# Reordering the first pooling, adaLN and first gate/up stages of a two-layer trunk on one NeuronCore

## The chip, the cores and the metric

The kernel is one program on one core of a Trainium2 chip. The metric is device time in microseconds of that core; lower is better. The time before is the median of three runs, 1387.15 us (1382.97 to 1387.4).

## The reference

The trunk has two layers over 256 tokens of width 1024. Only layer 0 up to its channel mixer matters here:

```python
mod_all = einsum('bd,lde->lbe', silu(c), w_mod) + b_mod        # 6 rows of 1024 per layer
shift1, scale1, gate1, shift2, scale2, gate2 = split(mod_all[0], 6)
h = rms_norm(x, g0) * (1 + scale1) + shift1
# pooling mixer: four groups of 256 channels, windows 2, 4, 8, 16 tokens
pooled = causal_window_mean(h, w) - h
y = (pooled @ w_grp) * pool_scale
x = x + gate1 * rms_norm(y, g1)
h = rms_norm(x, g2) * (1 + scale2) + shift2
y = swiglu(h, ffn_w_gu, ffn_w_down)                            # 1024 -> 2816 -> 1024
```

Layer 1 (differential attention, then eight experts of which two are taken) follows and is far the longer part. All values are float32. The large products are done as three passes over parts (high and low) whose sum is nearly float32.

## The kernel before, in words

Each engine runs an instruction list written out by hand, tied to the others by semaphores; there is no scheduler. Weights come through SyncE's queue (L487 to L571) in units of 128 x 2048 floats (1 MiB, two transfers of 512 KB) into a ring of six slots, `raw`; unit r may be loaded when unit r-6 has been used (`unit_done`, L451). The queue is strictly in order.

**The head.** Sixteen units (`HEAD`, L48) hold w_mod's columns for scale1 (units 0 to 3), shift1 (4 to 7), gate1 (8 to 11) and scale2 (12 to 15). VectorE multiplies each by silu(c), a value per partition, and adds it to a 128 x 1024 row sum (`head_units`, L1171: two instructions per unit). TensorE then sums over the partitions: for a column form (one value per channel on the partitions) by `column_sums` (L1683, eight products with a single moving column), for the gate's row form by two products with ones (L1764). shift2 does not pass VectorE: `shift_unit` (L1752) multiplies its four units on TensorE with silu(c) as a one-column weight, ScalarE copies the row out (L784), and eight one-column products turn it (L1785). In queue order the transfers are units 0 to 3, x (1 MiB), the pooling matrices `pool_m` (768 KB), units 4 to 7, `poolw` (1 MiB), units 8 to 11, shift2's unit 0, unit 12, shift2's units 1 to 3, units 13 to 15, then the first gate/up units 16 and 17.

**The pooling mixer.** ScalarE normalizes x (`normalize_tile`, L734). TensorE multiplies `ones` with the pooling matrices (L1712, L1713; for the shift) and the normalized x with them (L1725, L1728), eight column blocks in four banks. ScalarE scales each block out of its bank (L777), VectorE adds shift1 times the pooled ones over all 256 tokens (L1213, eight instructions of 128 x 256). GpSimd has meanwhile multiplied `poolw` by pool_scale in two instructions (L616). TensorE mixes (L1747, 32 passes), ScalarE squares, GpSimd makes the inverse roots (L606, L608), VectorE finishes the gate row (`finish_rows`, L1135) and adds to x (`residual_mixer`, L1150, L1155).

**Into the gate/up stage.** ScalarE squares and normalizes x again, TensorE turns both 128-token tiles (`turn`, L1772, eight transposes each). ScalarE modulates 512 of 2048 columns at a time (`modulate`, L790, with scale in `modc[:, 2]` and shift in `modc[:, 3]`), takes the high part (L798), and VectorE the low part (L1103). The first weight unit is split by halves between ScalarE (L788) and VectorE (L1251, L1253, L1257). `ffn_gate_up` (L1804) starts the long run of products, 96 for a step of 256 inner columns. `keep_clock` (L1678) issues products of zeros.

Of the kernel before, what the change touches and what calls it, by code (L numbers as in the profile page):

```python
# [8 lines left out]
ACT = mybir.ActivationFunctionType  # L9
AX_X = mybir.AxisListType.X  # L10
F32 = mybir.dt.float32
# [23 lines left out]
RAW = 6  # L35
SPL = 3
# [23 lines left out]
R_FFN, Q_FFN = len(HEAD), 0  # L60

# [58 lines left out]
def shape_constants():  # L120
# [31 lines left out]
def build_trunk(nc, x, c, w_mod, b_mod, norm_g, pool_w, pool_scale, w_qkv, w_o, subln_g, lambda_vecs,  # L152
# [8 lines left out]
    with ExitStack() as ctx:  # L161
# [102 lines left out]
        pool_m = scr[:, 0:4 * 384].rearrange("p (g s) -> p g s", g=4)  # L264
# [66 lines left out]
        first_lo = sem("first_lo")  # L331
        mcol_loaded = sem("mcol_loaded")
# [5 lines left out]
        m1_ps = sem("m1_ps")  # L338
# [106 lines left out]
        def _(sp):  # L445
# [47 lines left out]
            for r, (g, pair) in enumerate(HEAD):  # L493
# [83 lines left out]
        def _(pool):  # L577
# [54 lines left out]
            pool.wait_ge(col_ps, 5)  # L632
# [82 lines left out]
        def _(act):  # L715
            def high(r, q, rounds=0, qo=0):

                act.wait_ge(raw_loaded[r % RAW], 32 * (r // RAW + 1) + 32 * rounds)
# [60 lines left out]
            copy_wide(1, 6, gain[:, 1, :])  # L779
# [6 lines left out]

            act.wait_ge(raw_loaded[R_FFN % RAW], 32 * (R_FFN // RAW + 1))
            act.activation(whi[:, 0, 0:D], raw[:, R_FFN % RAW, 0:D], ACT.Copy).then_inc(hi_ready, 1)  # L788

# [68 lines left out]
            act.wait_ge(col_ready, 7)  # L858
# [31 lines left out]
            def project_high(u):  # L890
                act.wait_ge(raw_loaded[(R_WO + u) % RAW], 32 * ((R_WO + u) // RAW + 1))
# [76 lines left out]
            def expert_high(ps_no, m, e=0):  # L968

                r, q = R_MOE + ps_no * NE * EXPERT_UNITS + m, Q_MOE + ps_no * NE * EXPERT_UNITS + m  # L970
                act.wait_ge(raw_loaded[r % RAW], 32 * (r // RAW + 1) + 32 * (EXPERT_UNITS // RAW) * e)
# [115 lines left out]
        def _(dve):  # L1087
# [17 lines left out]
            def gemv_unit(r, l, g, cols, n, rounds=0, ro=0, no=0):  # L1105

                dve.wait_ge(raw_loaded[r % RAW], 32 * (r // RAW + 1) + 32 * rounds)
# [63 lines left out]
            def head_units(units):  # L1171

                for r in units:
                    g, pair = HEAD[r]
                    row = rows[:, ROW[0][g], :]
                    dve.wait_ge(raw_loaded[r % RAW], 32 * (r // RAW + 1))
# [27 lines left out]
            head_units(range(6, 8))  # L1204
# [3 lines left out]
            dve.wait_ge(m1_ps, 1)  # L1208
            for k in range(KC):
# [12 lines left out]
            dve.wait_ge(raw_loaded[last % RAW], 32 * (last // RAW + 1))  # L1222
# [11 lines left out]
            dve.wait_ge(col_ps, 3)  # L1234
            dve.tensor_tensor(modc[:, 3, :], ps[:, 0, 0:KC], cols[:, 3, :], ALU.add).then_inc(col_ready, 1)

            def scale_half(h):
# [5 lines left out]
                dve.tensor_tensor(modc[:, 2, a], modc[:, 4, a], cols[:, 7, a], ALU.mult).then_inc(col_ready, 1)  # L1243

            def low_modulated(b):
# [3 lines left out]
            scale_half(0)  # L1249
            dve.wait_ge(hi_ready, 1)  # L1250
            dve.tensor_tensor(wlo[:, 0, 0:D], raw[:, R_FFN % RAW, 0:D], whi[:, 0, 0:D].bitcast(F32), ALU.subtract).then_inc(first_lo, 1)  # L1251

            dve.tensor_copy(whi[:, 0, D:2 * D], raw[:, R_FFN % RAW, D:2 * D]).then_inc(first_hi, 1)  # L1253
            scale_half(1)
# [56 lines left out]
            dve.wait_ge(col_ps, 7)  # L1311
# [335 lines left out]
        def _(pe):  # L1647
# [592 lines left out]
```

## Time and profile before

| | us |
|---|---|
| median of three runs | 1387.15 |
| lowest, highest | 1382.97, 1387.4 |
| profiled execution, its own time | 1385.89 |
| its span in the trace | 1384.1 |
| TensorE / VectorE / ScalarE / GpSimd busy | 1350.9 / 1164.5 / 900.3 / 76.3 |
| chain that ended last | TensorE 94%, VectorE 3%, ScalarE 1%, transfers 1% |

The span is the time between first and last instruction in one profiled execution; the 1.79 us between it and the execution's own time lie around it. An engine's busy time counts its instructions only. The view of the chain follows the work back from the last instruction to what released each piece. The view of windows gives the busy time of each engine in a stretch, with the granted TensorE clock (1.00 is 2.4 GHz, 0.50 is 1.2 GHz) and what the transfers moved. A float32 product appears as two passes ("x2" for one product).

### The profile page before, as it was taken

Reading aid. Unit: us, or ns where it says so; the run is one execution under the profiler, and the core shown is the slowest. Engines: PE = TensorE matmul, PEld = TensorE weight load, DVE = VectorE, ACT = ScalarE, POOL = GpSimd, SP = SyncE. Lnnn points to the kernel's source line nnn. Section 1 sums busy time; section 2 is a strip of 40 time slices with the busy share of each in tenths; the row PEclk is TensorE's granted clock in tenths of the full one; section 3 lists DMA queues with packets and bytes.
Section 4 is the critical chain, followed back from the end, with each engine's and each line's share of the span. In section 5 each row is a group of like instructions: output and inputs, shape, how many; then the busy total and the mean of one; then the engine's idle time right before and its main releaser. Section 6 shows DMA issues by size and latency. Waiting matters only on the chain.

```text
span 1384.1 us, 19467 instructions
## 1 busy us (share of the span) xinstructions
PE 1350.9 (98%) x6873; PEld 1126.0 (81%) x6873; DVE 1164.5 (84%) x949; ACT 900.3 (65%) x748; POOL 76.3 (6%) x95
## 2 busy tenths in 40 slices
PE   6999999999899999999999999999999999999996
PEld 4499999898678888888888888888888888888885
DVE  6867778788869988888888888888888888898884
ACT  3353333556648777777777777777777777777772
POOL 3510000100210000000000000000000000000000
PEclk9899999999999999999999999999999999999998
DMA  9998889688259999999999999999999999999990
GB/s 363 407 343 284 309 310 338 241 284 324 100 181 348 411 393 359 391 379 381 363 392 393 347 400 377 378 362 390 385 347 405 381 367 379 383 387 351 412 354 33
DMA packets 210074, 475.14 MB, mean 343 GB/s; under 512 B 14976, under 2 KB 38608, under 8 KB 210016
## 3 DMA queue, kind: packets, MB, share of 16 engines
q1 hardware_dynamic: 204928, 457.76, 88.5%
q0 software_dynamic: 4944, 16.35, 3.9%
q8 instruction: 35, 0.57, 0.2%
q10 hardware_dynamic: 144, 0.26, 0.0%
q14 instruction: 23, 0.19, 0.0%
HBM read 465.39 MB, written 8.93 MB: 343 GB/s over the span
## 4 chain that ended last, share of the span: by engine, by line
PE 94%; DVE 3%; ACT 1%; DMA 1%; issue 1%; SPq 0%; DVEq 0%; POOL 0%
PE ps L1667 29%; PE ps L1669 28%; PE ps L1668 28%; PE ps L2119 2%; PE ps L1758 1%; DMA raw<-w_mod 1%; PE ps L1747 1%; PE ps L1685 1%; PE ps L1951 0%; DVE wlo L1443 0%; PE ps L2085 0%; PE ps L2076 0%; PE ps L1651 0%; DVE wlx L1443 0%; DVE hs L1392 0%
## 5 line engine op out<-in xcount | busy, mean ns | idle before, releaser
L1443 DVE TENSOR_TENSOR wlx<-raw,whx 128x2048 fp32r<-128x2048 f32 x168 | 384.8, 2292 | 97.5 <-ACT whx L980 96.7
L1443 DVE TENSOR_TENSOR wlo<-raw,whi 128x2048 fp32r<-128x2048 f32 x168 | 384.1, 2288 | 4.5 <-ACT whi L980 3.0
L980 ACT ACTIVATE whi<-raw 128x2048 fp32r<-128x2048 f32 x168 | 322.3, 1920 | 88.7 <-PE ps L1669 86.2
L980 ACT ACTIVATE whx<-raw 128x2048 fp32r<-128x2048 f32 x168 | 322.3, 1919 | 82.9 <-PE ps L1669 82.9
L1667 PE MATMUL ps<-whi,thi 128*128 128x512 f32 x516 | 207.9, 403 | 0.6 <-DVE tlo L1415 0.6
L1669 PE MATMUL ps<-whi,tlo 128*128 128x512 f32 x516 | 201.7, 391 | 0.0
L1668 PE MATMUL ps<-wlo,thi 128*128 128x512 f32 x516 | 201.3, 390 | 0.0
L1667 PE MATMUL ps<-whx,thi 128*128 128x512 f32 x460 | 179.9, 391 | 0.5 <-DVE tlo L1415 0.5
L1669 PE MATMUL ps<-whx,tlo 128*128 128x512 f32 x460 | 179.3, 390 | 0.0
L1668 PE MATMUL ps<-wlx,thi 128*128 128x512 f32 x452 | 176.0, 389 | 0.0
L1667 PE MATMUL ps<-thi,whi 128*128 128x256 f32 x480 | 136.4, 284 | 2.1 <-DVE tlo L1103 2.1
L1669 PE MATMUL ps<-thi,wlo 128*128 128x256 f32 x480 | 135.9, 283 | 0.0
L1668 PE MATMUL ps<-tlo,whi 128*128 128x256 f32 x480 | 135.9, 283 | 0.0
L1099 DVE TENSOR_TENSOR wlo<-raw,whi 128x2048 fp32r<-128x2048 f32 x44 | 99.8, 2289 | 37.5 <-ACT whi L722 37.5
L1667 PE MATMUL ps<-whi,ahi 128*128 128x512 f32 x300 | 118.1, 394 | 0.6 <-DVE alo L1103 0.6
L1669 PE MATMUL ps<-whi,alo 128*128 128x512 f32 x300 | 116.9, 390 | 0.0
L1668 PE MATMUL ps<-wlo,ahi 128*128 128x512 f32 x300 | 116.9, 390 | 0.0
L1667 PEld LDWEIGHTS ps<-whi,thi 128*128 128x128 f32 x516 | 97.0, 188 | 22.4 <-issue 2.8
L1669 PEld LDWEIGHTS ps<-whi,tlo 128*128 128x128 f32 x516 | 96.9, 188 | 21.1
L1668 PEld LDWEIGHTS ps<-wlo,thi 128*128 128x128 f32 x516 | 97.2, 188 | 18.6 <-issue 0.2
L722 ACT ACTIVATE whi<-raw 128x2048 fp32r<-128x2048 f32 x44 | 83.0, 1907 | 41.0 <-PE ps L1669 41.0
L1667 PEld LDWEIGHTS ps<-whx,thi 128*128 128x128 f32 x460 | 86.3, 188 | 20.8 <-issue 3.2
(286 smaller groups left out, 1914.2 us busy)
## 6 DMA issues: line engine op xcount, KB each, us to landing
raw<-moe_w_gu SPq DMA_DIRECT2D x448, 512.0 KB, 6.1
raw<-moe_w_down SPq DMA_DIRECT2D x224, 512.0 KB, 6.3
raw<-w_mod SPq DMA_DIRECT2D x88, 512.0 KB, 5.7
raw<-ffn_w_gu SPq DMA_DIRECT2D x44, 512.0 KB, 5.2
raw<-w_qkv SPq DMA_DIRECT2D x24, 512.0 KB, 5.4
raw<-ffn_w_down SPq DMA_DIRECT2D x22, 512.0 KB, 5.0
shift_w<-w_mod SPq DMA_DIRECT2D x8, 512.0 KB, 16.0
raw<-w_o SPq DMA_DIRECT2D x8, 512.0 KB, 5.7
```

The costliest lines, as they stand in the source:

```text
L722: act.activation(whi[:, q % SPL, :], raw[:, r % RAW, :], ACT.Copy).then_inc(hi_ready, 1)
L980: act.activation(m_hi[m % MRING], raw[:, r % RAW, :], ACT.Copy).then_inc(hi_ready, 1)
L1099: dve.tensor_tensor(wlo[:, q % SPL, :], raw[:, r % RAW, :], whi[:, q % SPL, :].bitcast(F32), ALU.subtract).then_inc(unit_done, 1)
L1443: dve.tensor_tensor(m_lo[m % MRING], raw[:, r % RAW, :], m_hi[m % MRING].bitcast(F32), ALU.subtract).then_inc(unit_done, 1)
L1667: pe.matmul(out, a_hi, b_hi, start=start, stop=False, skip_group_check=check)
L1668: pe.matmul(out, a_hi, b_lo, start=False, stop=False, skip_group_check=check)
L1669: return pe.matmul(out, a_lo, b_hi, start=False, stop=stop, skip_group_check=check)
L1685: mm = pe.matmul(out[:, k:k + 1], rows[:, ROW[l][g], k * P:k * P + P], ones[:, 0:1], start=True, stop=True)
L1747: mm = pe.matmul(ps[:, 4 + 2 * t + g // 2, (g % 2) * FC:(g % 2) * FC + FC], pooled_t[:, 2 * g + k, t * P:t * P + P], poolw[:, g, k, :], st ...
L1758: mm = pe.matmul(ps[0:1, 2 + h, :], silu_c[:, k:k + 1], shift_w[:, i, kk * D + h * 512:kk * D + h * 512 + 512], start=(k == 0), stop=(k == ...
L2119: mm = pe.transpose(ps[:, 6, jj * P:jj * P + P], actf[:, jj * P:jj * P + P], ident)
```

## The change

- The pooling matrices keep only what is needed: per window 160 columns (144 for the first tile's tokens and the 16 after it, 16 for the edge), 320 KB instead of 768 KB. A column block's pooling takes three products (144, 16 and 112 columns) instead of two (256 and 128). It no longer waits for the finished scale columns, only its last bank does, and the products of ones are moved behind it and cover 16 tokens per group.
- The pooled shift is added for the first 16 tokens only, since behind them a window's mean of a constant less the constant is zero.
- VectorE's small work for lambda and ScalarE's Exp move ahead; shift1's units follow in another order around the scale columns. Head unit 12 moves behind the residual.
- The spread of the first gain goes to banks 2 and 3 and ahead of the shift's sums. pool_scale is folded in eight instructions, by group.
- The gate's sum goes ahead of all four shift units. Both turns follow the shift; shift2's columns are made with scale2's, by halves.
- Unit 16 comes in four transfers of 256 KB by halves, ScalarE takes the high part of units 16 and 17 by halves, VectorE the low part by halves; VectorE's cast is gone. shift2's unit 3 is loaded behind head unit 13.

```diff
+REACH = 16
...
-    pool = np.zeros((P, len(WINDOWS), S + P), np.float32)
+    pool = np.zeros((P, len(WINDOWS), P + 2 * REACH), np.float32)
-        pool[:, g, 0:S] = full[0:P]
-        pool[:, g, S:] = full[P:, P:]
+        pool[:, g, 0:P + REACH] = full[0:P, 0:P + REACH]
+        pool[:, g, P + REACH:] = full[P:, P:P + REACH]
...
-                    for i in range(1, 4):
+                    for i in range(1, 3):
                         load_shift(i)
+                if r == 13:
+                    load_shift(3)
...
-            load(R_FFN, 0, gu_unit(w_gu, FF, 0, 0))
+            sp.wait_ge(unit_done, R_FFN - RAW + 1)
+            first_dst = raw[:, R_FFN % RAW, :].rearrange("p (k g j) -> p k g j", k=4, g=2)
+            first_src = w_gu.rearrange("(k p) (g f) -> p k g f", p=P, g=2)
+            for i in range(2):
+                for g in range(2):
+                    sp.dma_start(first_dst[:, 2 * i:2 * i + 2, g, :], first_src[:, 2 * i:2 * i + 2, g, 0:FC]).then_inc(first_loaded[i], 16)
             load(R_FFN + 1, 0, gu_unit(w_gu, FF, 0, 1))
...
-            for ch in range(2):
-                pool.tensor_tensor(poolw[:, :, ch, :], poolw[:, :, ch, :], rows[:, 6, :].rearrange("p (g e) -> p g e", g=4),
-                                   ALU.mult).then_inc(scale_folded, 1)
+            for g in range(4):
+                for ch in range(2):
+                    pool.tensor_tensor(poolw[:, g, ch, :], poolw[:, g, ch, :], rows[:, 6, g * FC:g * FC + FC],
+                                       ALU.mult).then_inc(scale_folded, 1)
...
             copy_wide(0, 2, rows[:, 6, :])
+            act.wait_ge(lam_prod, 2)
+            act.activation(lam[:, 2:4], lam[:, 0:2], ACT.Exp).then_inc(lam_exp, 1)
+            act.preload_act_table(ACT.Silu)
             square_x(0)
             for t in range(T):
                 normalize_tile(0, t)
-            act.wait_ge(lam_prod, 2)
-            act.activation(lam[:, 2:4], lam[:, 0:2], ACT.Exp).then_inc(lam_exp, 1)
-            act.preload_act_table(ACT.Silu)
...
-            copy_wide(1, 6, gain[:, 1, :])
+            copy_wide(1, 2, gain[:, 1, :])
...
-                act.wait_ge(col_ready, 4 + b // 2)
+                a = slice(b % 2 * D, b % 2 * D + D)
+                r = R_FFN + b // 2
+                if b < 2:
+                    act.wait_ge(first_loaded[b], 32)
+                else:
+                    act.wait_ge(raw_loaded[r % RAW], landed(r))
+                half = act.activation(whi[:, b // 2, a], raw[:, r % RAW, a], ACT.Copy)
+                if b % 2:
+                    half.then_inc(hi_ready, 1)
+                else:
+                    half.then_inc(first_hi, 1)
+                act.wait_ge(col_ready, 4 + 2 * (b // 2))
                 modulate(b)
                 high_modulated(b)
-                if b == 1:
-                    high(R_FFN + 1, 1)
...
-            head_units(range(0, 6))
-            dve.wait_ge(cols_ready, 1)
-            scale_columns(0, 1, ps[:, 7, 0:KC]).then_inc(col_ready, 1)
+            head_units(range(0, 3))
...
-            head_units(range(6, 8))
+            head_units(range(3, 5))
+            dve.wait_ge(cols_ready, 1)
+            scale_columns(0, 1, ps[:, 7, 0:KC]).then_inc(col_ready, 1)
+            head_units(range(5, 8))
...
-                dve.scalar_tensor_tensor(pooled_t[:, k, :], ps[:, 2 + g // 2, (g % 2) * S:(g % 2) * S + S], modc[:, 1, k:k + 1],
-                                         pooled_t[:, k, :], ALU.mult, ALU.add).then_inc(pooled_done, 1)
-            head_units(range(8, 13))
+                dve.scalar_tensor_tensor(pooled_t[:, k, 0:REACH], ps[:, 4, KC + g * REACH:KC + g * REACH + REACH], modc[:, 1, k:k + 1],
+                                         pooled_t[:, k, 0:REACH], ALU.mult, ALU.add).then_inc(pooled_done, 1)
+            head_units(range(8, 12))
             finish_rows(0, (2,))
             residual_mixer()
-            head_units(range(13, 15))
+            head_units(range(12, 15))
...
+            def half_columns(h):
                 a = slice(4 * h, 4 * h + 4)
-                dve.wait_ge(col_ps, 4 + h)
-                dve.scalar_tensor_tensor(modc[:, 4, a], ps[:, 1 + 2 * h, 0:4], 1.0, cols[:, 4, a], ALU.add, ALU.add).then_inc(col_step, 1)
+                dve.wait_ge(col_ps, 3 + h)
+                dve.scalar_tensor_tensor(modc[:, 4, a], ps[:, 1 + 2 * h, 4:8], 1.0, cols[:, 4, a], ALU.add, ALU.add).then_inc(col_step, 1)
+                dve.tensor_tensor(modc[:, 3, a], ps[:, 1 + 2 * h, 0:4], cols[:, 3, a], ALU.add).then_inc(col_ready, 1)
                 dve.wait_ge(col_step, 2 + h)
...
+            half_columns(0)
+            low_half(0, first_lo)
             low_modulated(0)
-            dve.wait_ge(first_hi, 1)
-            dve.tensor_tensor(wlo[:, 0, D:2 * D], raw[:, R_FFN % RAW, D:2 * D], whi[:, 0, D:2 * D].bitcast(F32),
-                              ALU.subtract).then_inc(unit_done, 1)
+            half_columns(1)
+            low_half(1, unit_done)
             low_modulated(1)
-            low(R_FFN + 1, 1)
+            low_half(2, first_lo)
             low_modulated(2)
+            low_half(3, unit_done)
             low_modulated(3)
...
-            pe.wait_ge(wide_ready, 1)
             pe.wait_ge(pool_loaded[0], 16)
-            for g in range(4):
-                b, c0 = 2 + g // 2, (g % 2) * S
-                pe.matmul(ps[:, b, c0:c0 + S], ones, pool_m[:, g, 0:S], start=(g % 2 == 0), stop=False, skip_group_check=True)
-                mm = pe.matmul(ps[:, b, c0 + P:c0 + S], ones, pool_m[:, g, S:S + P], start=False, stop=True, skip_group_check=True)
-            mm.then_inc(m1_ps, 1)
-            pe.wait_ge(dist_ready, 2)
-            pe.wait_ge(col_ready, 1)
             pe.wait_ge(h_ready, T)
             for b in range(4):
-                for t in range(T):
-                    for k in (2 * b, 2 * b + 1):
-                        c0 = (k % 2) * S
-                        g = k // 2
-                        if t == 0:
-                            mm = pe.matmul(ps[:, 4 + b, c0:c0 + S], hs[:, 0, k * P:k * P + P], pool_m[:, g, 0:S],
-                                           start=(k % 2 == 0), stop=False, skip_group_check=True)
-                        else:
-                            mm = pe.matmul(ps[:, 4 + b, c0 + P:c0 + S], hs[:, 1, k * P:k * P + P], pool_m[:, g, S:S + P],
-                                           start=False, stop=True, skip_group_check=True)
+                if b == 1:
+                    pe.wait_ge(dist_ready, 2)
+                elif b == 2:
+                    pe.wait_ge(cols_ready, 1)
+                elif b == 3:
+                    pe.wait_ge(col_ready, 1)
+                for k in (2 * b, 2 * b + 1):
+                    c0 = (k % 2) * S
+                    g = k // 2
+                    pe.matmul(ps[:, 4 + b, c0:c0 + P + REACH], hs[:, 0, k * P:k * P + P], pool_m[:, g, 0:P + REACH],
+                              start=(k % 2 == 0), stop=False, skip_group_check=True)
+                    pe.matmul(ps[:, 4 + b, c0 + P:c0 + P + REACH], hs[:, 1, k * P:k * P + P], pool_m[:, g, P + REACH:P + 2 * REACH],
+                              start=False, stop=False, skip_group_check=True)
+                    mm = pe.matmul(ps[:, 4 + b, c0 + P + REACH:c0 + S], hs[:, 1, k * P:k * P + P], pool_m[:, g, REACH:P],
+                                   start=False, stop=True, skip_group_check=True)
                 mm.then_inc(pooled_ps, 1)
...
+            pe.wait_ge(wide_ready, 1)
+            pe.wait_ge(first_gain_loaded, 16)
+            spread(1, 2)
+            pe.wait_ge(pooled_ready, KC)
+            for g in range(4):
+                pe.matmul(ps[:, 4, KC + g * REACH:KC + g * REACH + REACH], ones, pool_m[:, g, 0:REACH], start=True, stop=True)
             pe.wait_ge(unit_done, 8)
-            pe.wait_ge(pooled_ready, KC)
             column_sums(0, 0, ps[:, 4, 0:KC])
-            pe.wait_ge(first_gain_loaded, 16)
-            spread(1, 6)
-            pe.wait_ge(scale_folded, 2)
             for t in range(T):
                 if t == 0:
                     pe.wait_ge(col_ready, 2)
-                else:
-                    pe.wait_ge(wide_ready, 2)
                 for g in range(4):
-                    pe.wait_ge(pooled_done, 2 * g + 2)
...
-            shift_unit(0)
             pe.wait_ge(unit_done, 12)
             for h in range(2):
                 mm = pe.matmul(bank(ROW_BANK[0][2] + h), ones, rows[:, 2, h * 512:h * 512 + 512], start=False, stop=True)
             mm.then_inc(row_ps, 1)
-            for i in range(1, 4):
+            pe.wait_ge(wide_ready, 2)
+            for i in range(4):
                 mm = shift_unit(i)
             mm.then_inc(shift_ps, 1)
...
-            turn(0)
+            for t in range(T):
+                turn(t)
             pe.wait_ge(shift_copied, 1)
-            pe.wait_ge(row_done, done_rank(0, 2))
-            for k in range(KC):
-                mm = pe.matmul(ps[:, 0, k:k + 1], rows[0:1, 3, k * P:k * P + P], ones[0:1, 0:1], start=True, stop=True)
-            mm.then_inc(col_ps, 1)
             pe.wait_ge(zeros_ready, 1)
             keep_clock(2, 8)
-            turn(1)
-            keep_clock(2, 8)
+            pe.wait_ge(row_done, done_rank(0, 2))
             for h in range(2):
+                for k in range(4):
+                    pe.matmul(ps[:, 1 + 2 * h, k:k + 1], rows[0:1, 3, (4 * h + k) * P:(4 * h + k) * P + P], ones[0:1, 0:1],
+                              start=True, stop=True)
                 if h == 0:
                     pe.wait_ge(half_sum, 1)
                 else:
                     pe.wait_ge(unit_done, len(HEAD))
                 for k in range(4):
-                    mm = pe.matmul(ps[:, 1 + 2 * h, k:k + 1], rows[:, 4, (4 * h + k) * P:(4 * h + k) * P + P], ones[:, 0:1],
+                    mm = pe.matmul(ps[:, 1 + 2 * h, 4 + k:5 + k], rows[:, 4, (4 * h + k) * P:(4 * h + k) * P + P], ones[:, 0:1],
                                    start=True, stop=True)
                 mm.then_inc(col_ps, 1)
-            keep_clock(2, 24)
+            keep_clock(2, 16)
...
-                    if first and kh == 0:
-                        pe.wait_ge(first_lo, 1)
+                    if first:
+                        pe.wait_ge(first_lo, kh + 1)
```

In `ffn_gate_up` of the first step the waits go by halves of both units instead of by halves of the first.

## Rows read from the trace of the kernel before

**Rows 1.** Windows from 77 us: busy us (count) per engine, clock, DMA share, GB/s

```profile
77.00:1381.00 1304.00, 1288.42 (x6622) 1087.74 (x6622) 1110.04 (x887) 873.22 (x707) 41.45 (x51) 0.99 0.92 341
```

**Rows 2.** Windows inside the head, the same columns

```profile
34.40:38.40 4.00, 3.06 (x19) 2.59 (x20) 1.07 (x4) 0.79 (x2) 4.00 (x2) 0.97 1.03 420
...
38.40:45.00 6.60, 6.60 (x14) 4.11 (x14) 6.42 (x10) 1.01 (x1) 3.63 (x5) 0.50 1.04 396
...
68.80:72.20 3.40, 3.40 (x24) 3.34 (x22) 0.84 (x3) 0.26 (x1) 2.76 (x4) 0.51 1.09 385
```

**Rows 3.** Chain that ended last, by time, to 38 us: start, us, what

```profile
25.77 0.85 PE ps L1712 x2
...
28.84 1.10 PE ps L1725 x4
...
30.39 0.87 PE ps L1725 x4
...
34.35 0.85 ACT ysb L777 x2
...
35.34 1.92 PE ps L1685 x16
...
37.26 2.80 PE ps L1696 x4
```

**Rows 4.** Timeline to 41 us: start, us, engine, line, operation [idle before it]

```profile
19.43 3.57 PE L1685 MATMUL ps<-consts,rows 128*128 128x1 f32 x16 [0.82 <-DVE rows L1184]
...
21.27 2.19 ACT L737 ACTIVATE hs<-xs,rstd 128x1024 f32<-128x1024 f32 x2
...
33.10 1.28 DVE L1184 SCALAR_TENSOR_TENSOR rows<-raw,silu_c,rows 128x1024 f32<-128x1024 f32 x1
...
33.64 5.25 POOL L616 TENSOR_TENSOR scr<-scr,rows 128x1024 f32<-128x1024 f32 x2 [11.44 <-DMA scr<-pool_w]
...
37.49 3.23 DVE L1213 SCALAR_TENSOR_TENSOR ysb<-ps,modc,ysb 128x256 f32<-128x256 f32 x8
...
40.64 0.74 DVE L1182 TENSOR_SCALAR rows<-raw,silu_c 128x1024 f32<-128x1024 f32 x1
```

**Rows 5.** Chain, 40 to 66 us

```profile
40.06 9.54 PE ps L1747 x32
...
49.60 3.52 PE ps L1758 x8
...
53.12 1.91 PE ps L1766 x4
...
55.04 10.39 PE ps L1758 x24
```

**Rows 6.** Timeline of VectorE, 49 to 70 us

```profile
49.55 1.28 DVE L1184 SCALAR_TENSOR_TENSOR rows<-raw,silu_c,rows 128x1024 f32<-128x1024 f32 x1
...
55.08 1.23 DVE L1135 TENSOR_TENSOR rows<-ps,gain 128x1024 f32<-128x1024 f32 x1 [2.26 <-PE ps L1766]
...
68.85 0.75 DVE L1232 SCALAR_TENSOR_TENSOR rows<-raw,silu_c,rows 128x512 f32<-128x512 f32 x1
```

**Rows 7.** Chain, 65 to 78 us

```profile
65.46 1.10 PE ps L1777 x8
...
66.55 1.91 PE ps L1786 x16
...
70.76 0.85 PE ps L1681 x8
...
72.86 0.17 DVE modc L1241
...
76.39 0.61 DVE tlo L1103
...
77.14 0.36 PE ps L1667
```

**Rows 8.** Timeline of ScalarE at the first modulation

```profile
73.26 1.02 ACT L793 ACTIVATE tmp<-ps,modc 128x256 f32<-128x256 f32 x2 [4.20 <-DVE modc L1243]
```

More of the change, by code:

```diff
@@ L60, with landed @@
 R_FFN, Q_FFN = len(HEAD), 0
+def landed(r):
+    return 32 * (r // RAW + 1) - (32 if r % RAW == R_FFN % RAW and r >= R_FFN else 0)
 def ffn_steps():
@@ L331, in build_trunk @@
         first_lo = sem("first_lo")
+        first_loaded = [sem(f"first_loaded{i}") for i in range(2)]
         mcol_loaded = sem("mcol_loaded")
@@ L716, in high @@
             def high(r, q, rounds=0, qo=0):
-                act.wait_ge(raw_loaded[r % RAW], 32 * (r // RAW + 1) + 32 * rounds)
+                act.wait_ge(raw_loaded[r % RAW], landed(r) + 32 * rounds)
                 if q >= SPL - 1:
@@ L857, in _ @@
             square_residual(1)
-            act.wait_ge(col_ready, 7)
+            act.wait_ge(col_ready, 8)
             for t in range(T):
@@ L890, in project_high @@
             def project_high(u):
-                act.wait_ge(raw_loaded[(R_WO + u) % RAW], 32 * ((R_WO + u) // RAW + 1))
+                act.wait_ge(raw_loaded[(R_WO + u) % RAW], landed(R_WO + u))
                 if u:
@@ L970, in expert_high @@
                 r, q = R_MOE + ps_no * NE * EXPERT_UNITS + m, Q_MOE + ps_no * NE * EXPERT_UNITS + m
-                act.wait_ge(raw_loaded[r % RAW], 32 * (r // RAW + 1) + 32 * (EXPERT_UNITS // RAW) * e)
+                act.wait_ge(raw_loaded[r % RAW], landed(r) + 32 * (EXPERT_UNITS // RAW) * e)
                 if ps_no == 0 and m < SPL:
@@ L1105, in gemv_unit @@
             def gemv_unit(r, l, g, cols, n, rounds=0, ro=0, no=0):
-                dve.wait_ge(raw_loaded[r % RAW], 32 * (r // RAW + 1) + 32 * rounds)
+                dve.wait_ge(raw_loaded[r % RAW], landed(r) + 32 * rounds)
                 row = rows[:, ROW[l][g], :]
@@ L1175, in head_units @@
                     row = rows[:, ROW[0][g], :]
-                    dve.wait_ge(raw_loaded[r % RAW], 32 * (r // RAW + 1))
+                    dve.wait_ge(raw_loaded[r % RAW], landed(r))
                     if pair:
@@ L1207, in _ @@
             dve.wait_ge(col_ready, 2)
-            dve.wait_ge(m1_ps, 1)
             for k in range(KC):
@@ L1212, in _ @@
                 g = k // 2
-                dve.scalar_tensor_tensor(pooled_t[:, k, :], ps[:, 2 + g // 2, (g % 2) * S:(g % 2) * S + S], modc[:, 1, k:k + 1],
-                                         pooled_t[:, k, :], ALU.mult, ALU.add).then_inc(pooled_done, 1)
-            head_units(range(8, 13))
+                dve.scalar_tensor_tensor(pooled_t[:, k, 0:REACH], ps[:, 4, KC + g * REACH:KC + g * REACH + REACH], modc[:, 1, k:k + 1],
+                                         pooled_t[:, k, 0:REACH], ALU.mult, ALU.add).then_inc(pooled_done, 1)
+            head_units(range(8, 12))
             finish_rows(0, (2,))
             residual_mixer()
-            head_units(range(13, 15))
+            head_units(range(12, 15))
             last = len(HEAD) - 1
             row, unit = rows[:, 4, :], raw[:, last % RAW, :]
-            dve.wait_ge(raw_loaded[last % RAW], 32 * (last // RAW + 1))
+            dve.wait_ge(raw_loaded[last % RAW], landed(last))
             dve.wait_ge(unit_done, last)
@@ L1233, in _, with low_half @@
                                      ALU.mult, ALU.add).then_inc(unit_done, 1)
-            dve.wait_ge(col_ps, 3)
-            dve.tensor_tensor(modc[:, 3, :], ps[:, 0, 0:KC], cols[:, 3, :], ALU.add).then_inc(col_ready, 1)
-            def scale_half(h):
+            def half_columns(h):
                 a = slice(4 * h, 4 * h + 4)
-                dve.wait_ge(col_ps, 4 + h)
-                dve.scalar_tensor_tensor(modc[:, 4, a], ps[:, 1 + 2 * h, 0:4], 1.0, cols[:, 4, a], ALU.add, ALU.add).then_inc(col_step, 1)
+                dve.wait_ge(col_ps, 3 + h)
+                dve.scalar_tensor_tensor(modc[:, 4, a], ps[:, 1 + 2 * h, 4:8], 1.0, cols[:, 4, a], ALU.add, ALU.add).then_inc(col_step, 1)
+                dve.tensor_tensor(modc[:, 3, a], ps[:, 1 + 2 * h, 0:4], cols[:, 3, a], ALU.add).then_inc(col_ready, 1)
                 dve.wait_ge(col_step, 2 + h)
                 dve.tensor_tensor(modc[:, 2, a], modc[:, 4, a], cols[:, 7, a], ALU.mult).then_inc(col_ready, 1)
+            def low_half(b, done):
+                a = slice(b % 2 * D, b % 2 * D + D)
+                if b % 2:
+                    dve.wait_ge(hi_ready, b // 2 + 1)
+                else:
+                    dve.wait_ge(first_hi, b // 2 + 1)
+                dve.tensor_tensor(wlo[:, b // 2, a], raw[:, (R_FFN + b // 2) % RAW, a], whi[:, b // 2, a].bitcast(F32),
+                                  ALU.subtract).then_inc(done, 1)
             def low_modulated(b):
@@ L1741, in _ @@
                     pe.wait_ge(col_ready, 2)
-                else:
-                    pe.wait_ge(wide_ready, 2)
                 for g in range(4):
-                    pe.wait_ge(pooled_done, 2 * g + 2)
+                    pe.wait_ge(scale_folded, 2 * g + 2)
+                    pe.wait_ge(pooled_done, KC if t == 0 and g == 0 else 2 * g + 2)
                     for k in range(2):
@@ L1813, in ffn_gate_up @@
                         k = 4 * kh + kk
-                        if first and k == 2:
-                            pe.wait_ge(unit_done, r + 1)
+                        if first and kk == 2:
+                            pe.wait_ge(unit_done, r + kh + 1)
                         if first and k % 2 == 0:
```

16 lines of the change are left out of this document (4 added, 12 removed).

## The prediction, made before the changed kernel was run

> **What bounds the kernel now.** I read the windows first. From 77 us to the end TensorE is busy for 1288 of 1304 us at a granted clock of 0.99, with the transfers at 92% [rows 1]. No line after 77 us is edited except three semaphore numbers, so the change can only move the moment at which the first gate/up product starts, 77.14 us [rows 7], and how smoothly the first 96 products follow. The transfers have slack there (341 GB/s against the 420 they reach in the head [rows 1, 2]), and an earlier start should be kept to the end.
>
> The chain of waits is read next, since the head has no single owner. Up to 26 us the transfers and the sums paced by them lead; then pooling, column sums, the gain's spread and mixing on TensorE [rows 3, 5]; shift2's 32 passes with the gate's sum between them [rows 5]; turns and column products [rows 7]; and last VectorE, which splits a weight half and casts another before it may do tlo, and TensorE waits for that until 77.14 [rows 7]. The windows show what else is at work: TensorE's clock stands at 0.50 (1.2 GHz) from about 38.1 to 45.0 and again over 68.8 to 72.2 [rows 2]. Before the first fall TensorE had idled a little over a microsecond and then done 16 one-column passes and passes with a one-partition weight [rows 3]; before the second, eight transposes and 16 one-column passes [rows 7]. One more slow stretch is visible in durations only: at 25.77 two passes of 256 columns take 0.85 us, while from 28.84 four take 0.87 to 1.10 [rows 3]. So the first pooling products ran at 1.2 GHz and the later ones at 2.4.
>
> **The change part by part.** Times are those of the profiled execution, whose own time is 1385.89 us (span 1384.1), 1.26 below the median shown.
>
> *Pooling starts earlier.* Ones times the pooling matrices stood ahead of it on TensorE [rows 3]. Now it may start when ScalarE has normalized both tiles, 23.46 [rows 4], and the scale's column sums end: 19.43 + 3.57 = 23.0 [rows 4], plus about 0.4 for lambda's products, which now go ahead of unit 3. ScalarE's Exp and its two table loads move into its idle time before x lands and cost nothing; without that cover they would cost some 3 us. Start: 23.6 instead of 28.84.
>
> *Pooling gets longer.* No row shows a product of 16 columns. One-column passes cost 3.57/16 = 0.22 us slow and 1.92/16 = 0.12 fast [rows 3, 4], which is the weight load, and a 256-column pass 0.43 or 0.22. I take 0.12 for passes of 16 and 112 columns and 144 columns likewise; slow 0.22 to 0.24. 48 passes: 5.8 us fast, 11 slow (before: 5.5). With the clock rising at about 28, as it did, 4.3 us are slow and the rest fast: the end is at 31.4 instead of 34.3. Bounds: 29.4 and 34.6.
>
> *Spread, edge products, sums.* The spread (2.80, partly slow [rows 3]) is 1.7 fast and 3.4 slow; the new edge products are 8 passes, 1.0 or 1.8. Both stand ahead of shift1's column sums now. Unit 7, whose last sum ended at 34.38 [rows 4], comes about 1.1 us earlier with the smaller transfer, some 33.0, so it does not hold them. 31.4 + 1.7 + 1.0 = 34.1; sums 1.9 to 3.6: end 36.0 to 37.7 against 37.26. This is where most of the 5.2 us go: the queue of TensorE got longer ahead of VectorE's wait.
>
> *Shift on 16 tokens.* 3.23 us [rows 4] become eight instructions at the 0.17 us of a column instruction [rows 7], 1.4 us. No row has 16 columns from PSUM at this line: bounds 1.2 and 3.2. VectorE starts unit 8 at 39.1 instead of 40.64 [rows 4]: 1.5 us earlier.
>
> *Fold by group.* 5.25 us [rows 4] in eight parts; with a fixed price between 0 and 0.6 each it ends at 38 to 42. Mixing, 9.54 us before [rows 5], starts at 39.1 and ends at 47 to 49, ahead of unit 11 (49.3): hidden.
>
> *Gate's sum ahead.* Unit 12 leaves and shift_unit(0) no longer stands before the sum. Units 8 to 11 took 10.2 us, from 40.64 to the end of L1184 at 50.83 [rows 4, 6], and now end at 49.3. The sum runs at 49.3 to 51.3, so the gate row is made at 51.4 instead of 55.08 [rows 6], 3.7 us earlier; unit 12's 2.1 us are paid behind the residual. Units 13 to 15 so end 1.6 us earlier: 68.0 instead of 69.6 [rows 6]. The transfers allow it: pool_w landed at 33.64 [rows 4], now about 1.1 earlier (448 KB less at 410 GB/s); 12 units of 1.05 MB are loaded after it up to unit 15 in either kernel, 30.7 us, so unit 15 lands near 63.2 and is wanted at 65.0.
>
> *shift2.* TensorE does the same 36 passes as before, 3.52 + 1.91 + 10.39 = 15.8 us [rows 5], from 49.3 instead of 49.60: ready at 65.1 instead of 65.43. Only 0.3 us are won on the step that all the rest queues behind.
>
> *Behind it.* Row copied at 66.1; second tile normalized at 67.3 (it stands behind that copy on ScalarE), turned by 68.4; zeros 0.5; 16 one-column passes 1.9: 70.8 against 72.86 [rows 7]. Column arithmetic 0.5, modulation and high part 1.02 + 0.63 [rows 8], tlo 0.61 [rows 7], waits between them 0.3: first product at 73.9. The wlo half and the halves after it lie beside ScalarE's work, each half (1.04 and 1.22 us) shorter than the 2.9 us of 24 products. Against 77.14 this is 3.2 us.
>
> *TensorE's own queue.* Before that product it must still do the second half's 16 passes (1.9) and 16 products of zeros (1.0; [rows 7] show 0.85 for eight, slow): 70.8 + 2.9 = 73.7, just in time. But 32 one-column passes now stand in one block, where before 8 us held turns and zeros between two blocks of 16. Both falls shown came behind such passes. If the clock falls half-way, the rest costs 0.22 a pass and the zeros double: 1 to 1.5 us. I take 1.1.
>
> The sum: -3.2 + 1.1 = -2.1 us. Own time 1383.8; against the median 1385.0.
>
> A rule speaks against the new order. The Trainium skill (TensorE: Matmul & The Clock Gate, Part 4) says transposes do not count as work for the clock. The row at hand is mixed: over 68.8 to 72.2 TensorE did eight transposes and eight products of zeros, and the clock was back at 72.2. By that rule the two turns would not hold the clock and it would fall ahead of all 32 column passes; that is the second rival.
>
> **The rivals.** *The clock holds* and is up early in pooling: the 1.1 us are not paid, and up to 2 us more come from pooling, limited by unit 15's landing. -3.2 to -5.2: 1382.5. For it: one kernel's runs of 1383 and 1387 us leave room for a clock that falls at different places from run to run. *The clock falls before the column block:* 32 passes at 0.22 are 7.1 us from 68.9, zeros 2.0: 78.0, later than 77.14, and some slow products: 1388.5. For it: the fall at 68.8 with just such work; against: the second turn now comes right before. *The transfers hold:* units 14 and 15 come late because unit 16 asks four issues and unit 13 waits less; VectorE's end stays at 69.6: no gain, 1387. Against: 1.8 us of slack by the rate above. *Slower:* pooling's passes, a third of them 16 columns wide, do not raise the clock from 1.2 GHz. They stream for only about two thirds of the time, where the 256-column passes that stood there streamed all of it. Then pooling ends at 34.6, spread and edge 5.2 later, sums at 43.4; VectorE is 4.4 us later than before at unit 8 instead of 1.5 earlier, shift2 ends near 71, and the products start 5 us late: 1392. It decides when the clock is still low after 31 us.
>
> **How the numbers follow.** Forecast 0.35, clock holds 0.27, falls before the block 0.14, transfers 0.09, slower 0.15. A measurement can tell about 0.3%, 4.2 us. Below 1383.0 lie most of "holds" and a tail of the forecast: 0.30. Above 1391.3 lies "slower" with 0.14. Within: 0.56. The range leaves out that last case and reaches to 1380.8 (holds, with its best bound and a microsecond of scatter) and up to 1389.5.
>
> **What would show it.** Right: pooling from 23.6 with 0.12 us passes after a rise near 28 (a rise after 31 is the slower rival); VectorE's eight shift instructions under 1.5 us; L1135's successor near 51.4; shift2's last pass near 65; first gate/up product at 73.5 to 76. A window at 0.50 between 68 and 76 decides between forecast and rivals; a wait of VectorE for w_mod at units 14 or 15 speaks for the transfers. Wrong: gate/up products with gaps of over 0.5 us after the first, or a difference that arises after 90 us.

## The result, and the profile of the changed kernel

The changed kernel takes 1390.62 us (median of eight runs, 1389.5 to 1393.03), the kernel before in the same comparison 1385.66 us (median of eight, 1382.55 to 1387.4). The ratio is 1.0041, 95% interval 1.003 to 1.0052: slower by 0.4%, about 5 us. The forecast was 1385.0, 2.1 below the median of three that it started from; the range ended at 1389.5. So 2.1 us less were forecast, and 5 us more were measured.

The chain that ended last, in order of time: start, us, what. Pooling's first and last product, then what stands behind it.

```profile
23.61 0.82 PE ps L1748 x2
24.43 0.24 PE ps L1750 x2
24.66 0.59 PE ps L1752 x2
...
33.25 0.51 PE ps L1748 x2
...
34.59 3.71 PE ps L1723 x4
38.29 1.82 PE ps L1762 x8
40.11 3.41 PE ps L1712 x16
...
55.12 1.98 PE ps L1791 x4
57.11 13.84 PE ps L1784 x32
70.97 1.00 ACT rows L801
...
78.54 0.92 PE ps L1708 x16
79.56 0.36 PE ps L1694
...
81.07 0.21 PE ps L1695
...
92.79 0.91 PE ps L1701 x16
```

A column block costs 0.51 + 0.24 + 0.59 = 1.34 us once under way, the last (from 33.25 to 34.59) as well: the clock never leaves 1.2 GHz in pooling. That is read from durations: the column of the granted clock shows 1.00 here, as the last section says. The durations fit the level of 0.50: the column sums' one-column passes take 0.21 us each, and e4 shows 0.22 for such a pass in a window that does read 0.50. Pooling lasts from 23.61 to 34.59, as long as the slow bound had it. The spread then takes 3.71 (1.91 in e3, where the clock is up by then), the edge products 1.82, the column sums 3.41 where they took 1.92 [rows 3]. VectorE sees it as one wait. Its timeline, with the idle time before an instruction in brackets, first in the kernel before, then three lines of the changed one:

```profile
37.29 0.17 DVE L1206 TENSOR_TENSOR modc<-ps,cols 128x8 f32<-128x8 f32 x1 [2.91 <-PE ps L1685]
...
43.54 0.17 DVE L1229 TENSOR_TENSOR modc<-ps,cols 128x8 f32<-128x8 f32 x1 [10.99 <-PE ps L1712]
43.74 1.22 DVE L1235 SCALAR_TENSOR_TENSOR ysb<-ps,modc,ysb 128x16 f32<-128x16 f32 x8
44.88 0.74 DVE L1204 TENSOR_SCALAR rows<-raw,silu_c 128x1024 f32<-128x1024 f32 x1
```

Eleven idle microseconds stand where the kernel before had 2.9, and unit 8 begins at 44.88 instead of 40.64 [rows 4]. The gate row is made only 2.1 us late (57.15 against 55.08 [rows 6]), since its sum was moved ahead of shift2's passes. But all of these now wait for unit 11, and shift2's last pass ends 5.5 us late (70.95 against 65.43). Then the tail gives 3.1 us back: from the end of shift2's passes to the first gate/up product it takes 79.56 - 70.95 = 8.6 us, before 77.14 - 65.43 = 11.7 [rows 5, 7]. So that product is 2.4 us late. The windows (busy us and count of TensorE, its weight loads, VectorE, ScalarE, GpSimd, then granted clock, DMA share, GB/s) show the rest:

```profile
80.00:84.00 4.00, 4.00 (x24) 4.00 (x23) 3.05 (x4) 3.94 (x8) 0.90 (x2) 0.58 0.43 133
84.00:88.00 4.00, 4.00 (x36) 4.00 (x35) 2.75 (x6) 3.08 (x5) 0.73 (x2) 1.00 0.66 183
```

The clock falls right under the first gate/up products, which take 0.21 us each instead of 0.12. At the zeros behind the first step the delay is 92.79 - 88.89 = 3.9 us. The kernel before does the same 16 products in this line of its chain:

```profile
88.89 0.91 PE ps L1674 x16
```

The spans end 4.1 apart (1388.2, 1384.1), so nearly all of the loss arises before 93 us.

### The profile page after: what moved, and what is told of

It is laid out like the page before. It is cut to its first block, busy times and chain, and to the rows that moved or that the text cites. A ratio compares the mean times of both kernels' runs of the same rounds, so it can differ in the third digit from the quotient of the medians.

```text
span 1388.2 us, 19475 instructions
## 1 busy us (share of the span) xinstructions
PE 1355.4 (98%) x6865; PEld 1130.8 (81%) x6865; DVE 1161.8 (84%) x950; ACT 901.3 (65%) x750; POOL 73.6 (5%) x101
## 4 chain that ended last, share of the span: by engine, by line
PE 94%; DVE 3%; ACT 1%; issue 1%; DMA 0%; POOL 0%; DVEq 0%; POOLq 0%
PE ps L1694 29%; PE ps L1696 28%; PE ps L1695 28%; PE ps L2144 2%; PE ps L1784 1%; PE ps L1723 1%; PE ps L1712 0%; PE ps L1976 0%; DVE wlo L1470 0%; PE ps L2110 0%; DMA scr<-onehot_in 0%; PE ps L2101 0%; DVE rows L1206 0%; PE ps L1752 0%; DVE wlx L1470 0%
```

## The experiments

Times are medians; starts are those of the chain unless a timeline is named. "Before" in each is the kernel before on the same chip, 1385.5 to 1385.7 us throughout.

**One product for the second tile (e1).** From the changed kernel; the matrices are 544 KB.

```diff
-    pool = np.zeros((P, len(WINDOWS), P + 2 * REACH), np.float32)
+    pool = np.zeros((P, len(WINDOWS), 2 * P + REACH), np.float32)
-        pool[:, g, P + REACH:] = full[P:, P:P + REACH]
+        pool[:, g, P + REACH:] = full[P:, P:]
...
-                    pe.matmul(ps[:, 4 + b, c0 + P:c0 + P + REACH], hs[:, 1, k * P:k * P + P], pool_m[:, g, P + REACH:P + 2 * REACH],
-                              start=False, stop=False, skip_group_check=True)
-                    mm = pe.matmul(ps[:, 4 + b, c0 + P + REACH:c0 + S], hs[:, 1, k * P:k * P + P], pool_m[:, g, REACH:P],
+                    mm = pe.matmul(ps[:, 4 + b, c0 + P:c0 + S], hs[:, 1, k * P:k * P + P], pool_m[:, g, P + REACH:2 * P + REACH],
                                    start=False, stop=True, skip_group_check=True)
```

> The changed kernel, but the second tile's 16 and 112 columns are one product of 128, so that no pooling pass is narrower than 128 columns (matrices of 544 KB instead of 320 KB). Theory (narrow passes leave the array idle a third of the time, so the clock stays at 1.2 GHz through pooling): the clock rises within the pooling block, four passes of a column block drop from 0.9 us to about 0.5, pooling ends near 30 to 31 instead of 34.6, shift1's sums end by 39 instead of 43.5, and the time falls by 3 to 5 us against the changed kernel, to 1386 or less. Rival (the products of ones that stood ahead had warmed the clock, width has nothing to do with it): the clock stays low as long as before, pooling ends at 31 by fewer passes (32 x 0.23 = 7.4 us from 23.6) with passes at 0.22 to 0.24 to the end, the spread still takes 3.7, sums end near 40, time 1387 to 1388.

Measured: 1384.31 us, 6.3 less than the changed kernel; against the kernel before the ratio is 0.9991 (0.998 to 1.0002), no difference. TensorE's timeline, in pooling and behind it:

```profile
26.36 0.69 PE L1748 MATMUL ps<-scr,hs 128*128 128x144 f32 x2
...
27.27 0.42 PE L1748 MATMUL ps<-scr,hs 128*128 128x144 f32 x2
...
28.21 0.41 PE L1748 MATMUL ps<-scr,hs 128*128 128x144 f32 x2
28.46 0.38 PE L1750 MATMUL ps<-scr,hs 128*128 128x128 f32 x2
28.68 0.41 PE L1748 MATMUL ps<-scr,hs 128*128 128x144 f32 x2
...
29.25 1.98 PE L1723 MATMUL ps<-tmp,consts 1*128 1x512 f32 x4
...
33.14 2.72 PE L1712 MATMUL ps<-consts,rows 128*128 128x1 f32 x16 [0.92 <-DVE rows L1206]
```

A column block takes 0.47 us from 28.21 to 28.68. The clock rose at about 27.2, inside pooling, which ends at 29.2. The spread takes 1.9, and the sums now wait for unit 7 on VectorE, not VectorE for them. The theory holds and its rival (the missing products of ones alone) falls: nothing stands ahead of pooling here either. The gain is above the 3 to 5 us expected. e6, e7 and e9 pool in the same way, and there too the clock rises inside pooling, at about 28.9, 28.3 and 29.6; in the changed kernel and in e2, with the narrow products, it does not. What e1 does not separate is the width from the number of passes, 32 instead of 48 over the same 272 columns a block. Fewer passes at 1.2 GHz, 32 x 0.23 from 23.6, would have ended at 31.

**The spread behind the sums (e2).** From the changed kernel; `spread(1, 2)` moves behind `column_sums(0, 0, ...)`.

> The changed kernel with the gain's spread behind shift1's column sums instead of ahead of them. Theory (the queue ahead of VectorE's wait is what costs, 3.7 us of it the spread at 1.2 GHz): VectorE gets shift1's columns 3.7 us earlier, near 39.8, unit 11 ends near 51.4, shift2's passes end near 67.3, time 3 to 4 us less, 1387. Rival (mixing then becomes the wait: spread and mixing stand one behind the other at 1.2 GHz): mixing starts at 43.5 instead of 45.1, and ends near 53, later than unit 11, so only 1 to 2 us are won, 1389.

Measured: 1389.58 us, 1.0 less; ratio to before 1.0037 (1.0021 to 1.0053). Its chain:

```profile
37.34 3.39 PE ps L1712 x16
40.73 3.70 PE ps L1723 x4
44.44 8.93 PE ps L1773 x32
53.37 1.72 PE ps L1791 x4
55.09 13.84 PE ps L1784 x32
```

The rival was right on the mechanism. The sums end at 40.7, 2.8 earlier, but mixing starts only when the spread is done, ends at 53.37 and holds the gate's sum. shift2's last pass ends at 68.93, 2.0 earlier, and at the zeros behind the first step 0.7 are left (92.06 against 92.79). The 1.0 us between the medians is less than the comparison can tell (the intervals overlap). The order of the queue does not bring the 5 us back, and pooling is as slow as in the changed kernel.

**Zeros ahead of pooling (e3).** From the changed kernel; narrow passes stay.

```diff
             pe.wait_ge(pool_loaded[0], 16)
+            pe.wait_ge(wide_ready, 1)
+            pe.wait_ge(zeros_ready, 1)
+            keep_clock(2, 24)
             pe.wait_ge(h_ready, T)
```

> The changed kernel with 24 products of zeros (128 columns each) between the scale's column sums and pooling. They cost 2.6 to 3.1 us at 1.2 GHz, so pooling starts near 26. Theory (the missing products of ones had raised the clock; once up it holds): pooling's 48 passes take 0.12 each in the main, it ends near 32.5, sums by 38, time 2 to 4 us less than the changed kernel. Rival (narrow passes do not hold it either, they stream for two thirds of the time): the clock stays low or falls again, pooling ends at 35 to 37, and the time is 0 to 3 us more than the changed kernel.

Measured: 1385.55 us median of ten runs, one of them 1392.55; ratio to before 1.0015 (1.0001 to 1.0029). That is 5 us less than the changed kernel. TensorE's timeline:

```profile
22.72 2.72 PE L1708 MATMUL ps<-zeros 128*128 128x128 bf16 x24
25.24 0.80 PE L1751 MATMUL ps<-scr,hs 128*128 128x144 f32 x2
...
30.37 0.42 PE L1751 MATMUL ps<-scr,hs 128*128 128x144 f32 x2
...
31.06 0.42 PE L1751 MATMUL ps<-scr,hs 128*128 128x144 f32 x2
```

From 27.3 on a block takes 0.69 us (30.37 to 31.06) instead of 1.34, and pooling, begun 1.8 us later, ends 2.7 earlier, at 31.9. Once up, the clock stays up through four microseconds of narrow passes. So here they do not drop it within their stretch, and without the zeros they did not raise it. Behind the spread it does fall: the edge products take 1.62 and the sums 3.40, ending at 38.84 and not by 38. The gain of 5 us is nevertheless above the 2 to 4 expected. The one execution at 1392.55 took as long as those of the changed kernel; whether the zeros failed to raise the clock in it is not shown, as it has no trace.

**The old pooling stage with the new tail (e4).** From the changed kernel: ones times the full matrices, 256 and 128 columns, shift on 256 tokens, spread behind the sums; the gate's sum ahead, unit 12 behind the residual, turns, columns by halves and weight halves stay.

> The changed kernel with the old pooling stage: ones times the full matrices first, 256 and 128 columns, shift on all 256 tokens, spread behind the sums. What stays is the gate's sum ahead, unit 12 behind the residual, both turns behind the shift, columns and weight halves. Theory (all of the loss lies in the pooling stage, and the rest won its 3 us): shift1's sums end near 37.3 and unit 11 at 50.8 as in the kernel before, shift2's passes end near 66.5 (the gate's sum now waits 1 us for unit 11), first gate/up product near 75, time 1382 to 1385, below the kernel before by 1 to 3 us. Rival (the tail gained nothing net, since its 32 one-column passes lower the clock under the first gate/up products): equal to the kernel before within 1 us, 1385 to 1386.

Measured: 1386.27 us; ratio to before 1.0007 (0.9996 to 1.0018). The rival was right: no gain. The first half of the theory held too: with the old pooling stage back, the 5 us of the changed kernel are gone, so its loss lies in that stage. Chain and windows:

```profile
51.88 13.84 PE ps L1788 x32
65.74 1.00 ACT rows L802
...
71.35 1.18 PE ps L1821 x8
72.53 1.80 PE ps L1828 x8
74.33 1.73 PE ps L1710 x16
76.06 0.32 PE ps L1696
...
88.88 0.91 PE ps L1703 x16
```

```profile
72.00:76.00 4.00, 4.00 (x28) 3.98 (x29) 3.07 (x6) 3.94 (x8) 1.61 (x1) 0.50 1.07 402
76.00:80.00 4.00, 4.00 (x25) 4.00 (x25) 3.13 (x4) 3.97 (x7) 0.68 (x2) 0.65 1.07 386
```

shift2's passes end 0.3 later than before (65.72 against 65.43), since the gate's sum waits 3 us for unit 11 (from 46.9 to 49.90) with nothing to do in between. The first gate/up product comes at 76.06, 1.1 earlier, and at the zeros behind the first step both kernels are level, 88.88 and 88.89. The clock falls at about 72, inside the second half of the 32 one-column passes (1.18 and 1.80 us for eight, 0.98 before), and stays at 1.2 GHz through the zeros and the first dozen of the step's 96 products, to 78.7.

**Zeros between the halves (e5).** From e4, `keep_clock(2, 8)` behind the first half's columns.

> The run with the old pooling stage and the new tail, plus 8 products of zeros between the two halves of the column products (16 products of zeros still stand behind them). There, the 32 one-column passes were followed by a clock of 1.2 GHz for 6.8 us, from 71.9 to 78.7, over the zeros and the first gate/up products. Theory (this fall is what takes back the tail's gain): the clock stays up or falls for half as long, the first gate/up product comes by 75 and its successors at 0.12 us, and the time is 1 to 2 us below that run, 1384.5 to 1385. Rival (8 zeros are too few to matter, 0.5 us of them only lengthen TensorE's queue): the same fall, time equal or 0.5 us more.

Measured: 1387.47 us median of 12 runs (1382.33 to 1389.04); ratio to before 1.0007 (0.9995 to 1.002), the same as for e4. In its chain the second half's passes still take 1.54 and 1.80 and the last zeros 1.73: the clock falls all the same, and the first gate/up product comes at 76.76, 0.7 later than in e4. Eight zeros do not prevent it; the rival was right. Whether more would was not run.

**Normalization ahead of the copy (e6).** From e1, ScalarE's `normalize_tile(1, 1)` ahead of `act.wait_ge(shift_ps, 1)`.

> The changed kernel with the second tile's pooling in one product of 128 columns (as in the run called wide) and with ScalarE's second normalization ahead of the copy of shift2's row instead of behind it. In that run TensorE idled 1.1 us between the two turns for it. Theory (the chain behind shift2 runs copy, normalization, turn): second turn right behind the first, the first column products 1.1 us earlier, near 66.6, first gate/up product near 71.9, time 1 us below that run, 1383.3. Rival (the last head unit takes over: it is summed at 66.0, held by transfers, and the clock falls under the column products at another place): gain under 0.5 us, or given back by slow products.

Measured: 1383.3 us; ratio to before 0.9986 (0.9975 to 0.9998). It is 1.0 below e1, which the comparison cannot tell apart from nothing (the intervals overlap). Its chain:

```profile
50.75 13.82 PE ps L1782 x32
64.57 1.91 PE ps L1802 x16
```

Both turns now follow shift2's passes without a gap. In this execution the sums of shift1 were slow again (3.40 us from 33.60), so all stands 0.6 later than in e1 and the first gate/up product is at 73.38. Counted from the end of shift2's passes it comes 0.35 us earlier than in e1 (8.81 against 9.16 us), and the zeros behind the first step come no earlier (21.87 against 21.61), since more products run at 1.2 GHz. So the turn moved as the theory said, but the trace speaks for the rival: the gain was given back by slow products.

**Zeros in idle time as well (e7).** From e6, 16 products of zeros ahead of shift1's column sums and 8 between the halves.

> As the run before it, plus 16 products of zeros in the idle time ahead of shift1's column sums and 8 between the halves of the column products in the tail. Theory (the clock's falls are set by stretches of one-column passes, and zeros in idle time break them): mixing runs at 2.4 GHz, the first gate/up products too; mixing is hidden ahead of unit 11, so only the tail's part counts, 1 to 1.5 us below the run without zeros, about 1382. Rival (the falls only move to other places): no difference beyond 0.5 us.

Measured: 1382.92 us; ratio to before 0.9983 (0.9974 to 0.9993). That is 0.4 below e6, less than the comparison can tell, so the rival stands: shift1's sums are fast (1.99 us), but the clock falls at their end (0.50 from 36 to 40 us, under the start of mixing), and the first gate/up products still meet 1.2 GHz.

```profile
72.00:76.00 4.00, 4.00 (x27) 4.00 (x26) 3.69 (x7) 3.94 (x7) 2.19 (x2) 0.50 1.06 408
```

**Narrow passes behind the products of ones (e8).** From the kernel before; only the pooling products change, three per block, out of the old matrices.

> The kernel before with one part of the change alone: each column block pooled by three products (144, 16 and 112 columns), behind the products of ones that stay ahead of it. Theory (narrow passes cost only their weight loads once the clock is up, 12 passes of 0.12 per bank; the loss in the changed kernel is that they do not raise it): the clock is up at 28 as before, pooling lasts 5.8 us instead of 5.5, the time is that of the kernel before within 0.7 us. Rival (narrow passes are bad at any clock: they let it fall): the clock falls in or right behind pooling, shift1's sums take 3.5 us instead of 1.9 and end near 39.5, time 1 to 3 us over the kernel before.

Measured: 1386.23 us; ratio to before 1.0011 (1.0 to 1.0022). Pooling ran at 2.4 GHz from 28.6 to 34.4:

```profile
33.39 0.30 PE ps L1727 x2
34.08 0.32 PE ps L1727 x2
34.42 0.85 ACT ysb L777 x2
35.40 2.26 PE ps L1685 x16
```

Blocks 0.69 us apart (33.39 to 34.08), ScalarE released at 34.42 against 34.35 [rows 3]. The theory holds for the stage: warm, the third product is nearly free. It is not shown to be free for the kernel. The clock fell inside the sums in this execution (2.26 us instead of 1.92), the spread took 3.70 instead of 2.80, and mixing ended 1.7 later, at 51.30. The first gate/up product still came at 77.20, but the clock fell under the products behind it (it reads 0.72 from 76 to 80 us), and the zeros behind the first step came at 90.42, 1.5 late. The profiled execution took 1387.72, 1.5 above the median, so it is one of the slower ones.

**shift2's columns by transposes (e9).** From e7 without the zeros between the halves:

```diff
-                    pe.matmul(ps[:, 1 + 2 * h, k:k + 1], rows[0:1, 3, ...], ones[0:1, 0:1], start=True, stop=True)
+                    pe.transpose(ps[:, 1 + 2 * h, k:k + 1], rows[0:1, 3, ...], ident[0:1, 0:1])
```

> As the run with both kinds of zeros, without the zeros between the halves, and shift2's eight column products are transposes with one element of the identity instead of products with a one: one pass each instead of two, so the block of one-column passes has 24 instead of 32. Theory (length of that block sets both the time of the scale's first half and the fall of the clock under the first gate/up products): first half's columns 0.5 us earlier, near 67.7, TensorE's queue 1.4 us shorter than with the zeros, first gate/up product near 71 to 72, time 0.5 to 1.5 us below that run, 1381.5 to 1382.4. Rival (the first product waits for scale, modulation and tlo anyway, and unit 15 is summed at 66.0): only 0 to 0.5 us.

Measured: 1382.73 us; ratio to before 0.9983 (0.9974 to 0.9992), equal to e7. By time the rival (0 to 0.5 us) is right. TensorE's timeline shows the shorter block, and a product still under 1.2 GHz behind it:

```profile
68.20 0.40 PE L1818 MATMUL ps<-consts,rows 1*128 1x1 f32 x4
68.53 1.05 PE L1824 MATMUL ps<-consts,rows 128*128 128x1 f32 x8
...
72.67 0.56 PE L1694 MATMUL ps<-thi,whi 128*128 128x256 f32 x1
```

Four transposes take 0.4 us where eight passes took 0.98. In this execution, though, the zeros ahead of shift1's sums fell into a slow stretch and held the sums until 35.2, so its first product, at 72.92, has to be counted from the end of shift2's passes: 7.0 us, against 9.6 in e7, and 19.0 against 22.3 to the zeros behind the first step. The tail did get shorter in this trace as the theory said; a possible reason why the medians do not show it stands under what stays open. e6, e7 and e9 are the versions whose interval lies below the kernel before, e7 and e9 by 2.5 to 2.9 us; these two are 7.7 to 7.9 below the changed one.

## Why the prediction was wrong, point by point

**The step that failed** is *Pooling gets longer*, with its sentence "With the clock rising at about 28, as it did". The passes cost what the step said for 1.2 GHz (1.34 us for a block's six, 0.22 each), but the clock did not rise, and the end came at 34.59, the bound of 34.6. In the kernel before the clock rose at 27.9, while the products of ones, 256 and 128 columns wide, still stood in front of pooling; the change both took those away and made their successors narrow. e1 and e3 each put one thing right, width or warm-up, and each won back 5 to 6 us. The forecast had pooling end at 31.4, 3.2 us earlier than it did, and what stands behind it on TensorE paid the low clock too. With this the step is the whole miss up to shift2: unit 8 was forecast for 39.1 and began at 44.88, 5.8 later, and shift2's last pass was forecast for 65.1 and ended at 70.95, 5.85 later. The rival *Slower* named this mechanism, with pooling's end at 34.6 and the sums' at 43.4; they came at 34.59 and 43.52. It had a chance of 0.15, as its only evidence was an estimate that the passes stream two thirds of the time. Its price, 1392, was 1.4 too high.

**What went with it.** *Spread, edge products, sums* was given as 1.7 + 1.0 + 1.9 to 3.6; its slow values (3.4, 1.8, 3.6) came true as 3.71, 1.82 and 3.41. That the longer queue ahead of VectorE's wait costs most of the early start was right in direction; e2 prices its order at 1 us, since mixing waits in its place, and not clear of noise.

**What held.** Start at 23.6 (23.61). Shift on 16 tokens 1.4 us (1.22 for eight). The fold hidden. Units 8 to 11 in 10.2 us (44.88 to the sum's start at 55.12). shift2 as the step that all queues behind: its last pass ends at 70.95. Behind it 8.8 us to the first product without the clock's price (8.6). In e1, where pooling is fast, VectorE waited 0.67 us for w_mod at unit 14: there the slack of the transfers, given as 1.8 us, is used up.

**TensorE's own queue.** The 1.1 us for a fall under the column passes were near in size, and that is luck: in the changed kernel the column passes ran at 2.4 GHz, and the fall came later, under the first gate/up products, and took 1.5 us (3.9 less 2.4). e4 shows 1.1 us gained at the first product and all of it given back by the end of the first step. e5 and e7 show that 8 zeros do not prevent it. The rule of the Trainium skill (TensorE: Matmul & The Clock Gate, Part 4), that transposes do not count as work, decided nothing: the clock did not fall behind the two turns but some 6 us later, after all 32 column passes. No run isolates a transpose.

**What stays open.** Which property of the narrow passes keeps the clock down (their width, their number, the share of time in which they stream) is not separated, and the changed kernel's own level in pooling was seen in two traces, its own and e2's.

An early start is not always kept to the end. From the zeros behind the first step to the end of the span, eight traces take 1295.2 to 1295.6 us, but e1, e5 and e9 take 1297.2, 1297.0 and 1296.8. These three have a longer stretch at 1.2 GHz far behind the edits, around a block of 32 one-column passes (L1685, from 266.65 in the timeline of the kernel before). The windows of the kernel before and of e1:

```profile
255.00:285.00 30.00, 29.88 (x143) 23.67 (x142) 18.25 (x19) 20.11 (x36) 3.71 (x9) 0.94 0.45 154
255.00:285.00 30.00, 30.00 (x138) 24.06 (x137) 16.00 (x16) 19.62 (x34) 3.72 (x9) 0.89 0.39 125
```

The granted clock reads 0.94 there in the eight and 0.89 in the three. So e1 was 3.3 us ahead of the kernel before at 86 us (85.60 against 88.89), and its span ended 1.3 ahead; e9 was 1.3 ahead of e7 at 85 us and ended 0.4 behind. Whether a stage that starts earlier meets the longer stretch by its timing or by chance is not known; the medians contain it, and no run was made to remove it.

## What to carry to other kernels

When a matmul block is moved forward or trimmed, ask what had raised the clock for it, and whether its successor still would: in e3 and e8 narrow passes cost little while the clock was up, and in the changed kernel eleven microseconds of them did not raise it. Read the slow price of a whole stage, not of one block, since everything behind it on TensorE pays it too. Eleven microseconds at half speed outweighed 448 KB and 2 us of vector work saved.

## What the runs showed that was not expected

The granted clock read 1.00 in every window from 20 to 76 us of the changed kernel, while one-column passes took 0.22 us and two passes of 144 columns 0.51:

```profile
28.00:32.00 4.00, 4.00 (x20) 4.00 (x20) 3.82 (x4) 0.88 (x3) 0.00 (x0) 1.00 1.07 397
```

In these traces the clock's column is right only from its first fall on: the rise inside e1's pooling is missing from it as well. Up to that fall the pass durations tell the level. The line shows one more thing: the weight loads (the second busy time) fill all four microseconds. The other surprise is the asymmetry: the same narrow passes ran at 2.4 GHz for four to six microseconds in e3 and e8, and at 1.2 GHz for eleven without a rise in the changed kernel.
